# Issuing the experts' down weights from ScalarE's own DMA queue in a one-core decoder layer

## What is computed

```
for g in range(N_EXPERT_GROUPS):
    hg = jnp.einsum('nd,edf->nef', x, w_gate[g])
    hu = jnp.einsum('nd,edf->nef', x, w_up[g])
    a = jax.nn.silu(hg) * hu * gate[:, g, :, None].astype(x.dtype)
    y = y + jnp.einsum('nef,efd->nd', a, w_down[g]).astype(jnp.float32)
```

## Time and profile before

| | |
|---|---|
| runs | 1011.37, 1013.74, 1012.26 us; median 1012.26 |
| profiled execution | 1013.08 us in all, span 1011.3 us (first to last instruction) |
| granted clock of TensorE over the span | 0.952 |
| TensorE busy | 906.9 us (90%) |
| VectorE busy | 553.9 us (55%) |
| ScalarE busy | 410.1 us (41%) |
| q1 (SyncE's queue) | 247.97 MB, its packets 67.8% of the 16 DMA engines' time |
| q0 (GpSimd's queue) | 24.66 MB, 6.9% |

### The profile page before, as it was taken

One profiled execution on the slowest core, in us unless ns is written; L12 is line 12 of the kernel. 1 busy time (PEld: TensorE's weight loads), 2 busy tenths in 40 slices (PEclk: granted clock), 3 DMA queues, 4 the chain that ended last, 5 costly groups with the idle time before them and its releaser, 6 DMA issues.

```text
span 1011.3 us, 13331 instructions
## 1 busy us (share of the span) xinstructions
PE 906.9 (90%) x5132; PEld 644.8 (64%) x5132; DVE 553.9 (55%) x1023; ACT 410.1 (41%) x748; POOL 135.6 (13%) x83
## 2 busy tenths in 40 slices
PE   6999999986999999769999835999999999999684
PEld 6999879953555545437888524666666666656331
DVE  5202020049566665683554367676767676767248
ACT  5202020033564555471222122646465555546145
POOL 0000000140000000000000002254545321121100
PEclk9999999998999999988999955999999999999987
DMA  9999999198686666409722291899999999997293
GB/s 350 328 346 338 375 351 348 56 391 244 215 327 236 244 235 225 167 1 359 244 89 68 77 385 48 301 358 372 358 358 352 358 354 371 361 360 274 83 381 130
DMA packets 54847, 273.49 MB, mean 270 GB/s; under 512 B 13984, under 2 KB 16544, under 8 KB 39680
## 3 DMA queue, kind: packets, MB, share of 16 engines
q1 hardware_dynamic: 46016, 247.97, 67.8%
q0 software_dynamic: 8768, 24.66, 6.9%
HBM read 256.33 MB, written 95.30 MB: 348 GB/s over the span
## 4 chain that ended last, share of the span: by engine, by line
PE 77%; DVE 11%; DMA 5%; ACT 3%; issue 3%; SPq 0%; POOLq 0%; DVEq 0%; ACTq 0%
PE psum L636 69%; PE psum L695 4%; PE psum L874 2%; DMA back<-w_gu 2%; DMA front<-w_gu 2%; DVE back L1222 1%; DVE front L1232 1%; DVE front L1233 1%; DVE front L1579 1%; ACT back L490 1%; DVE stats L1207 1%; DVE back L1204 1%; PE psum L834 1%; ACT back L986 1%; DMA middle<-pair_d 1%
## 5 line engine op out<-in xcount | busy, mean ns | idle before, releaser
L636 PE MATMUL psum<-back,front 128*64 128x128 f32 (+1 forms) x896 | 148.6, 359 | 7.7 <-ACT back L490 4.4
L1645 POOL DMA_INDIRECT pair_d<-front,back x32 | 84.1, 2628 | 200.4 <-ACT front L1097 143.2
L636 PEld LDWEIGHTS psum<-back,front 128*64 128x64 f32 (+1 forms) x896 | 70.3, 148 | 62.9 <-issue 53.7
L636 PE MATMUL psum<-gu_high,xg_high 128*112 128x512 f32 x256 | 104.3, 407 | 2.1 <-DVE xg_low L1472 2.1
L636 PE MATMUL psum<-gu_high,xg_low 128*112 128x512 f32 x256 | 102.0, 399 | 0.0
L636 PE MATMUL psum<-x_high,w_high 128*128 128x352 f32 x288 | 94.2, 327 | 8.3 <-DVE w_low L361 8.3
L636 PE MATMUL psum<-gu_low,xg_high 128*112 128x512 f32 x256 | 101.5, 397 | 0.0
L636 PE MATMUL psum<-front 64*128 64x256 f32 (+5 forms) x384 | 91.5, 494 | 10.8 <-DVE stats L1204 10.1
L636 PE MATMUL psum<-x_low,w_high 128*128 128x352 f32 x288 | 93.5, 325 | 0.0
L636 PE MATMUL psum<-x_high,w_low 128*128 128x352 f32 x288 | 93.5, 325 | 0.0
L490 ACT COPY back<-psum 128x512 f32<-128x512 f32 (+1 forms) x88 | 46.9, 547 | 85.5 <-PE psum L695 85.3
(11 more groups left out here) (199 smaller groups left out, 1626.4 us busy)
## 6 DMA issues: line engine op xcount, KB each, us to landing
out_win_k_s<-cache_win_k SPq DMA_DIRECT2D x16, 2044.0 KB, 13.7
out_win_v_s<-cache_win_v SPq DMA_DIRECT2D x16, 2044.0 KB, 12.6
back<-w_down SPq DMA_DIRECT2D x24, 1024.0 KB, 14.3
front<-w_gu SPq DMA_DIRECT2D x22, 1024.0 KB, 11.9
middle<-w_gu SPq DMA_DIRECT2D x22, 1024.0 KB
back<-w_gu SPq DMA_DIRECT2D x20, 1024.0 KB, 14.4
back<-winkT SPq DMA_DIRECT2D x8, 1792.0 KB, 7.6
back<-cache_win_v SPq DMA_DIRECT2D x8, 1024.0 KB, 7.2
```

Of the source, the lines that this page charges most:

```text
L636: return nc.tensor.matmul(out, lhsT, rhs, start=start, stop=stop, skip_group_check=True)
L1645: G.indirect_dma_start(pair_d, bass.IndirectOffsetOnAxis(ap=IDX[0:CAP, NE + e:NE + e + 1], axis=0), YS[e % 2][0:CAP, :], None, bounds_chec ...
```

## The change

`load_dn(e)` for e = 4 to 31 leaves SyncE together with its wait, and ScalarE issues it, right after `y_half(e - 4)`, which has waited for the same event (`down(e - 4)` done). The loads of experts 0 to 3 stay with SyncE.

```diff
@@ block.sync
                 for half in range(2):
                     sp.wait_ge(s_gu, 2 * (e - 3) + half + 1)
                     load_gu(sp, e, half)
-                if e >= 4:
-                    sp.wait_ge(s_y, e - 3)
-                    load_dn(sp, e)
@@ block.scalar
                 if e:
                     y_half(e - 1)
+                    if e + 3 < NE:
+                        load_dn(act, e + 3)
```

## The result

The changed kernel takes 1021.1 us (median of 4 runs, 1020.5 to 1022.1) against 1011.8 us before in the same comparison: a ratio of 1.0094, 95% interval 1.007 to 1.0117. That is 9.3 us slower. The direction was forecast, the size was not: 1015.2 us, with a range up to 1018.2. The profiled execution took 1022.1 us with a span of 1020.3, so 9.0 us of span against the one of before.

The account below looks back on a forecast made before the run. The prediction took TensorE to set the loop's pace at first and the DMA engines later. Its terms, 0 + 0 + 0 + 2.9 us, on the median 1012.3 gave 1015.2 us, with a range of 1011.0 to 1018.2.

Parts of the forecast that it names:

- What bounds the kernel: Loop over experts: TensorE sets the pace first at 9.97 us per iteration, DMA later; DMA costs 3.9 us in all.
- SyncE, 0: On SyncE, 28 issues of 0.33 us and their waits go; worth 0.
- ScalarE's issue, 0: Issuing on ScalarE takes 0.33 us, at most 1.07, hidden by idle time or 1.6 us of slack; cost 0.
- Rival 3: The issue holds ScalarE past 1.6 us, delaying `gate_up` in DMA-bound iterations: about 1018 to 1022 us; chance 0.04.
- The passing: On its own queue a down load goes past waiting gate and up weights, which land 2.9 us later: cost 2.9 us.
- rival 1: The order in which DMA serves loads stays in effect the same, so nothing moves: 1012.3 us; chance 0.19.
- From there on an iteration takes 10.54 instead of 9.97: From the load at 802.2 us, DMA sets the pace 4 to 5 iterations sooner, at 0.57 us each: 2.3 to 2.9 us.
- The total bytes are the same, so the loss does not grow beyond that.: Loop's end: the last binding half lands one down load later, +2.9 us; TensorE then runs at its own pace.
- `load_dn` would be issued some 6 us later: DMA-bound part of the loop: down weights are needed some 30 us or more after issue, so later issue is worth 0.
- The signs that the prediction listed: Changed profile: 802 us second halves after about 18 us, TensorE's first `y_half` wait near 800, DMA share and GB/s as before.
- Rival 2: A second hardware queue keeps DMA engines better fed; 2.5% more rate leaves no DMA-bound iteration: 1008.4 us; chance 0.12.

Follow-up runs that it names:

- `e_light`: Changed kernel, but down loads of experts 4 to 31 bring only the first half of their rows (0.5 MB): 1007.5 us, ratio 0.9957.
- `e_fine`: Changed kernel with each ScalarE down load cut by columns into four pieces (128 partitions x 2 KB each): 1019.1 us, ratio 1.0068.
- `e_one_more`: Kernel before, plus one additional 1 MB transfer in SyncE's queue at expert 10, once: 1014.5 us, ratio 1.0023.
- `e_last`: Kernel before, but ScalarE issues the down loads of experts 18 to 31, SyncE those up to 17: 1018.8 us, ratio 1.0055.
- the halves: Changed kernel with each ScalarE down load cut by columns in two (128 partitions x 4 KB each): 1019.3 us, ratio 1.0073.
- `e_between`: Changed kernel, ScalarE's down-load issue moved between the two halves of `weights_rounded`, ahead of the wait for the second half: 1018.2 us, ratio 1.0063.
- `e_first`: Kernel before, but ScalarE issues the down loads of experts 4 to 17, SyncE those of 18 to 31: 1013.8 us, ratio 1.001.
- `e_coupled`: Kernel before, one queue, but SyncE issues expert e's down load only once expert e - 1's second half has landed: 1013.1 us, ratio 1.001.
- the queue kernels: Only the 96 expert weight loads: one queue, 6 outstanding, 244.3 us; two queues, 4 and 2 outstanding, 244.2 us.

## Why the prediction was right or wrong

**What bounds the kernel: right.** The 3.9 us that DMA costs in the kernel before were read correctly; `e_light` recovers 4.2.

**SyncE, 0: right.** Nothing in the loop waits on it.

**ScalarE's issue, 0: right.** The row is 0.34 us. It even runs before `y_half`: it starts 0.1 us after the landing, where the prediction had 2.7 us, while the last two roundings are still to be done, and `y_half` starts 1.9 us after the landing in both kernels (813.91 - 812.00, and 862.60 - 860.7). Rival 3 did not occur in the changed kernel; in `e_fine` it did, through a full queue, which the prediction had not thought of.

**The passing: right in kind, and 2.9 us is about its size.** Down loads land after 11.2 us instead of 18.6, though not after the 6 to 9 that were forecast:

```profile
back<-w_down ACTq DMA_DIRECT2D x5, 1024.0 KB, 11.2
```

One transfer of delay costs 2.2 us in `e_one_more`. The delay of expert 11's second half grew by 5.2 us against the profiled execution of before (15.2 and 10.0), but that execution was an early one. In `e_last`, whose instructions are those of before up to there, it is 12.1 us, and the difference is 3.1. The Trainium skill's page on DMA ("DMA: Bandwidth & Descriptors", "Queues, rings and completion order") has engines drain a packet from one queue before they change to the next. The fine cut agrees: in pieces of a quarter, a down load no longer passes gate and up (8.2 us); the halves (20 us) do not show it. What the Trainium skill says in the same page's section "Issuing engines are not separate DMA queues", by which issuing from several engines only saves issue time (rival 1), holds for the rate (244.3 and 244.2 us) but says nothing of the landings, and these moved here (11.2 instead of 18.6 us).

**The step that failed: "From there on an iteration takes 10.54 instead of 9.97", and "The total bytes are the same, so the loss does not grow beyond that."** It took for granted that a DMA-bound iteration keeps its price, with the engines at the rate of the earlier trace rows. The runs showed 10.78 us and 342 to 345 instead of 360 GB/s, and 15 such iterations where some 11 were forecast. In the prediction's own terms, the excess over 9.97 us per iteration was 3.9 us before, was forecast as 3.9 + 2.9 = 6.8, and measured 14.1. The difference of 10.2 us between the profiled loops divides like this:

- more iterations at the old price, 15 x (10.54 - 9.97) - 3.9 = 4.6 us, where 2.9 were forecast;
- a longer period, (10.78 - 10.54) x 15 = 3.6 us, forecast as nothing;
- the one `down` at 1.2 GHz, 1.7 us, forecast as nothing. Such a row, 5.36 us, stands in the profile of `e_last` too, but none in that of before;
- 0.3 us that these terms leave over.

The loop also began 1.2 us earlier in this execution (642.20 instead of 643.40), which makes the 9.0 us of span.

**Why the rate fell is only in part known.** The prediction saw that `load_dn` would be issued some 6 us later, and costed this at nothing because nobody waits for down weights. The explanation that fits most runs is that the engines do. Before, SyncE hands over a down load as soon as `down` is done, and that load lies in the same queue behind gate and up, work for whichever engine is ahead. After, the next down load is issued by a ScalarE that stands at `weights_rounded` until the slowest engine has delivered a second half. Engines that are ahead can find both queues empty: 0.67 to 0.72 for a microsecond in each period. For it speak `e_between` (earlier issue, a third of the loss back, though the intervals overlap) and `e_last` against `e_first` (mostly where DMA sets the pace). Against it as the whole cause speak two measurements: from 842 to 918 us the busy share fell by one point and the rate by 4.4%, and `e_coupled` has engines idle for longer and loses 1.3 us. What makes a packet of q1 take 0.334 instead of 0.317 us stays open; the second queue beside GpSimd's is the rival that was not excluded. Nor is it settled why `e_between` still loses 5.9 us, of which the passing accounts for 2.2, and which engines lag, since the profile does not name them.

**The signs that the prediction listed.** Second halves at 802 us were to land after about 18 us and landed after 20.5; TensorE's first wait was to come near 800 us and came at 792; DMA share and GB/s were to stay and fell. This last sign is the one that shows that a part of the mechanism was missing.

**Rival 2** (more rate from two queues) did not come true: the queue kernels show no gain (244.3 and 244.2 us), and in the loop the rate fell. That a rate can also fall had no place among the rivals.

## What to carry to other kernels

When DMA sets the pace, put a load in the queue of an engine that does not stand at a landing, in the order in which its data are needed. Here a second queue added no bandwidth and let what had time (down loads, 11.2 instead of 18.6 us) overtake what had none. Costing a moved DMA takes two questions: who waits for its data, and whether the rate that the sum takes for granted still holds once the issue comes later and from another queue. Pricing one delay at the old rate gave less than a third of the loss here (2.9 of 9.3 us). And a queue that is served last can fill up and hold the engine that issues to it (6.00 us in `e_fine`), so a busy compute engine is a poor owner for it.

## What was not expected of the hardware

- A load of 1 MB in four pieces of 32 partitions took the loop from 362 to 240 GB/s at a DMA share of 0.96, and the kernel from 1011.7 to 1133.1 us; four pieces of 128 partitions x 2 KB did not (364 GB/s from 700 to 720 us).
- An issue on ScalarE, 0.34 us when its queue has room, took up to 4.1 us for one of the 256 KB pieces in `e_fine` once the queue was behind.
- DMA alone moved 422 GB/s in loads of 1 MB; with 17% more bytes on GpSimd's queue the whole took 45% longer (354.2 against 244.3 us), at a busy share of 1.02.
